# A two-layer encoder step on one core: GpSimd decodes the picks of the first two units, part of the projections is written beside the first dots, and the modulation weights are spread through the first attention

## The chip, the cores and the metric

The kernel runs on one core of a Trainium2 chip. The metric is the device time of one execution in microseconds. Five engines work side by side, each on its own list of instructions in order: TensorE (PE), VectorE (DVE), ScalarE (ACT), GpSimd (POOL) and SyncE (SP), which here does nothing but issue transfers. They wait for one another through semaphores.

## What is computed

Two encoder layers over 512 prompt rows and 64 sample rows, width 1024. The first layer has latent attention, the second band attention; each is followed by an expert layer in which every row picks 128 of 16384 experts (8 heads, 16 each). The parts that matter here:

```python
mod = silu(c) @ ada_w[layer] + ada_b[layer]          # shifts, scales, gates of every norm
q = rmsnorm(c_q @ w_uq);  k, v = from ckv_all @ w_ukv # 16 heads
x = x + g_m * (softmax(q k^T) v @ w_o)

def peer_ffn(h, w_q, subkeys, u, v):                  # once per 128 rows and layer
    q = (xb @ w_q).reshape(128, 8, 2, 64)
    s = einsum('nhpe,hpke->nhpk', q, subkeys)         # 128 scores per half
    top_s, top_i = lax.top_k(s, 16)                   # per head and half
    cand_s = top_s[:, :, 0, :, None] + top_s[:, :, 1, None, :]   # 16 x 16
    best_s, best_pos = lax.top_k(cand_s, 16)
    idx = take_along_axis(cand_i, best_pos)           # the expert's number
    g = softmax(best_s)
    a = gelu(einsum('nd,nhkd->nhk', xb, u[idx]))
    return einsum('nhk,nhkd->nd', g * a, v[idx])
```

## The kernel before

**Units.** The rows fall into five tiles (the sample's 64 rows first, then four prompt tiles of 128), and a tile in a layer is a unit: units 0 to 9. Each unit goes through attention (`attention`), the scores of the experts (`select`, `prepare`), the choice of the experts on DVE (`choose`), 64 (sample) or 128 gathered rows of `u` with one dot product each on DVE (`gather_u` on POOL into four slots of 0.5 MB, `dot` on DVE), and as many gathered rows of `v`, which PE adds up (`gather_v`, `add_values`). A gather may be issued when the dot that used its slot four rows earlier is done.

**Steady stages.** From the end of the ramp on, stage by stage, the dots of one unit stand beside the values of the unit before, the choice of the next and the attention of the one after.

**The ramp.** What comes before that is ordered by `RAMP` (line 54), a string that every engine walks through letter by letter. Each letter names a generator; an engine runs its next piece of that generator, if it has one. The letters are: l, one 2 MB piece of the modulation weights `ada_w` (PE multiplies it, line 626; DVE adds biases after each fourth, line 1481); Q, the queries of the sample; a, b and h, the attentions of units 0, 1 and 2 (some 17 pieces of one head, and the output product after each second head, line 847); s and r, the expert scores of units 0 and 1; p, the projections to queries, keys and values of the blocks n = 3 to 6 (blocks 0 to 2 come before the ramp), eight pieces each; c and k, the choice for units 0 and 1; e and f, the exponentials for it; d, the 64 dots of unit 0; t, the turning of its expert numbers. `RAMP` has five parts: modulations and first attention, its scores, choice beside projections, dots beside the second attention, dots beside the choice of unit 1.

**The choice.** `choose` does per head: the best 16 of two times 128 scores and of their 256 sums (`choose_head`, lines 1636 to 1648, three pieces of some 2 us). After two heads `decode` turns the 32 positions into expert numbers: it splits them (lines 1662 to 1665), then for each half compares them with `iota`, multiplies by the table of indices and sums (lines 1669, 1672, 1673: three instructions over 128 x 512). After four heads `name_experts` makes the list from which POOL gathers.

**The modulation weights.** `ada_w` comes in 28 pieces of 2 MB; 12 to 27 (the late ones) share two slots. SP issues piece p when piece p - 2 has been multiplied (`pieces`, a wait for `ada_used`). SP's list holds `pieces(12, 23)`, then the loads of the first attention. That attention's loads go by pairs of heads g: `keys(g+2)`, `values(g+1)`, `out_rows(g)` (0.5 MB of the output weights), and behind each of g = 0 to 4 one piece more, 23 to 27. The keys have two rings: `keys(g+2)` may be issued when the scores of pair g are done. All SP's transfers, these and the pieces, run in one queue (q1).

**Gathers.** POOL first stores the latents of the five tiles as they come (lines 1961, 1962), waits until all latents are multiplied (the gathered rows take the place of `w_in`), and then only gathers.

## Time and profile before

| | us |
|---|---|
| median of 3 runs | 4176.54 (4174.93 to 4184.52) |
| the profiled execution, its own time | 4168.8 |
| span of its trace | 4166.9 |

| engine | busy us | share of the span |
|---|---|---|
| PE | 2633.7 | 63% |
| DVE | 2452.3 | 59% |
| POOL | 2448.0 | 59% |
| ACT | 452.8 | 11% |

The transfers moved 1478 MB, 355 GB/s on average; the gathers' queue q0 alone had 75% of the sixteen DMA engines' time. How to read it: no engine is busy all the time, and the share of the transfers is an average over stages that differ much. So the stretches are looked at one by one.

### The profile page before, as it was taken

To read this page: it belongs to the slowest core of one execution; us is meant where nothing else is said; L and a number is where in the kernel's file an instruction comes from. 1 tells how busy PE (TensorE), PEld (TensorE's weight loads), DVE (VectorE), ACT (ScalarE), POOL (GpSimd) and SP (SyncE) were. 2 spreads that over 40 slices of the span, in tenths; PEclk is the share of its full clock that TensorE was granted. 3 is DMA by queue.
4 is the path that set the end of the run, shared out by engine and by line. 5 is a ranking of instruction groups with operands and counts; after the bars stand their busy time and mean duration, and the time that the engine had idled before them with its cause. 6 is when DMAs were issued, how large, how long until landed. Compare 5 with 4: busy or idle time off the path is not lost.

```text
span 4166.9 us, 31596 instructions
## 1 busy us (share of the span) xinstructions
PE 2633.7 (63%) x9649; PEld 958.8 (23%) x9649; DVE 2452.3 (59%) x5936; ACT 452.8 (11%) x1097; POOL 2448.0 (59%) x2323
## 2 busy tenths in 40 slices
PE   6587854664564455655465765656464677767789
PEld 2144532221222111211121222222121321111122
DVE  2119687786666556755773665677557667754410
ACT  2124411110010000110011011011001110000000
POOL 0000145777776757775676565556666677777776
PEclk8788866786787676767667877878686899999999
DMA  9761677999998999998998998899899999999999
GB/s 350 272 228 51 199 253 234 357 370 347 388 395 340 379 403 395 394 379 352 406 400 333 393 392 332 344 376 368 333 411 409 399 385 409 405 410 408 409 410 371
DMA packets 482966, 1478.16 MB, mean 355 GB/s; under 512 B 61568, under 2 KB 135248, under 8 KB 482128
## 3 DMA queue, kind: packets, MB, share of 16 engines
q0 software_dynamic: 332160, 1208.77, 75.0%
q1 hardware_dynamic: 125056, 255.33, 16.6%
q10 hardware_dynamic: 25584, 12.06, 1.0%
q8 instruction: 79, 1.29, 0.1%
q14 instruction: 87, 0.71, 0.0%
HBM read 1448.97 MB, written 28.57 MB: 355 GB/s over the span
## 4 chain that ended last, share of the span: by engine, by line
DMA 34%; POOL 23%; PE 18%; DVE 14%; issue 10%; ACT 1%; SPq 1%; ACTq 0%; DVEq 0%; POOLq 0%
DMA A<-in_uv,A 30%; POOL A L1930 12%; POOL A L1950 11%; PE P L939 8%; DVE A L1753 6%; DMA A<-in_ada_w 3%; PE P L847 2%; PE P L626 1%; PE P L881 1%; PE P L817 1%; PE P L687 1%; DVE A L1640 1%; DVE A L1637 1%; DVE A L1448 1%; PE P L804 1%
## 5 line engine op out<-in xcount | busy, mean ns | idle before, releaser
L939 PE MATMUL P<-A 128*32 128x512 f32 x4608 | 1314.2, 811 | 1185.5 <-DMA A<-in_uv,A 1117.5
L1930 POOL DMA_INDIRECT A<-in_uv,A x1152 | 1217.5, 1057 | 832.4 <-DVE A L1753 580.7
L1753 DVE CUSTOM_DVE_ANT_0 A<-A 128x1024 f32<-128x1024 f32 x900 | 1093.9, 1224 | 773.9 <-DMA A<-in_uv,A 766.4
L1950 POOL DMA_INDIRECT A<-in_uv,A x1152 | 1220.2, 1059 | 444.9 <-issue 320.2
L939 PEld LDWEIGHTS P<-A 128*32 128x32 f32 x4608 | 268.7, 132 | 2046.3 <-issue 1584.4
L1753 DVE CUSTOM_DVE_ANT_0 A<-P,A 128x1024 f32<-128x1024 f32 x252 | 307.8, 1224 | 263.0 <-DMA A<-in_uv,A 261.9
L956 PE MATMUL P<-A 128*128 128x512 f32 (+1 forms) x480 | 230.8, 627 | 18.5 <-DMA A<-in_w_kv 11.6
L817 PE MATMUL P<-A 128*128 128x128 f32 (+2 forms) x832 | 152.1, 317 | 87.1 <-DVE A L1603 82.6
L1961 POOL DMA_DIRECT2D out_ckv_p<-A x4 | 2.2, 548 | 333.9 <-DVE A L1528 333.9
L847 PE MATMUL P<-A 128*128 128x512 f32 (+1 forms) x320 | 190.9, 727 | 1.9 <-DMA A<-in_w_oA 1.3
L804 PE MATMUL P<-A 96*64 96x320 f32 (+9 forms) x320 | 148.5, 564 | 28.2 <-DMA A<-kBp_scratch 13.0
L831 PE MATMUL P<-A 128*64 128x128 f32 (+2 forms) x832 | 134.1, 295 | 38.2 <-ACT A L1263 38.1
L817 PEld LDWEIGHTS P<-A 128*128 128x128 f32 (+2 forms) x832 | 119.8, 210 | 154.9 <-DVE A L1603 98.6
L881 PE MATMUL P<-A 128*128 128x512 f32 x288 | 131.7, 612 | 0.0
L1271 ACT COPY A<-P 128x128 f32<-128x128 f32 (+3 forms) x160 | 62.7, 392 | 609.7 <-PE P L817 609.0
L956 PEld LDWEIGHTS P<-A 128*128 128x128 f32 (+1 forms) x480 | 85.9, 189 | 176.5 <-issue 127.8
L626 PE MATMUL P<-A,cs 128*32 128x512 f32 x448 | 76.9, 822 | 65.8 <-DMA A<-in_ada_w 65.8
L831 PEld LDWEIGHTS P<-A 128*64 128x64 f32 (+1 forms) x832 | 92.0, 150 | 69.3 <-issue 54.4
L1448 DVE TENSOR_SCALAR A<-P,gain,modT 128x128 f32<-128x128 f32 (+1 forms) x160 | 50.6, 389 | 79.8 <-PE P L606 79.8
L1636 DVE MAX8 A<-A 128x8 f32<-128x128 f32 (+1 forms) x240 | 80.5, 336 | 27.3 <-ACT A L1319 24.0
L804 PEld LDWEIGHTS P<-A 64*128 64x128 f32 (+3 forms) x320 | 55.5, 220 | 177.1 <-issue 169.0
L1753 DVE DVE_READ_ACCUMULATOR2_ANT A<- 128x1 f32 x1152 | 94.8, 82 | 0.0
(177 smaller groups left out, 2127.5 us busy)
## 6 DMA issues: line engine op xcount, KB each, us to landing
A<-in_ada_w SPq DMA_DIRECT2D x28, 2048.0 KB, 9.3
A<-in_w_kv SPq DMA_DIRECT2D x80, 512.0 KB, 8.6
A<-in_uv,A POOLq DMA_INDIRECT x2304, 7.8
A<-in_w_oA SPq DMA_DIRECT2D x40, 512.0 KB, 7.0
A<-in_w_q SPq DMA_DIRECT2D x40, 512.0 KB, 8.2
A<-in_w_oB SPq DMA_DIRECT2D x40, 512.0 KB, 7.9
A<-in_p_w_q SPq DMA_DIRECT2D x2, 4096.0 KB, 15.8
G<-mod_scratch SPq DMA_DIRECT2D x8, 512.0 KB, 7.6
```

The source lines that it names most:

```text
L626: ins = pe.matmul(P[32 * q:32 * q + 32, mods_bank(g), :], csT[:, c, :], slot[:, q, ADA_BLOCK * (c % 2):ADA_BLOCK * (c % 2 + 1)], start=(c ...
L804: ins = pe.matmul(P[0:r, n % 2, 0:nk], lhs, rhs, start=True, stop=not masked, skip_group_check=True)
L817: ins = pe.matmul(P[0:size, 2, b * 128:b * 128 + r], probs[m % 2][0:r, b * 128:b * 128 + size], turner[m % 2][0:r, 0:r], start=True, stop= ...
L831: ins = pe.matmul(P[p0:p0 + 64, 3, 0:r], V[0:size, b, p0:p0 + 64], probT[m % 2][0:size, b, 0:r], start=(b == 0), stop=(b == len(bl) - 1), ...
L847: ins = pe.matmul(P[0:r, 4 + b, :], oT[:, c, 0:r], w_o[pair % 2][:, 512 * b:512 * b + 512], start=(c == 0), stop=(c == C - 1), skip_group_ ...
L881: ins = pe.matmul(P[:, b, :], hT[:, c, :], w_pq[:, c, 512 * b:512 * b + 512], start=(c == 0), stop=(c == C - 1))
L939: ins = pe.matmul(Y[32 * j:32 * j + 32, b, :], spread[:, w:w + STRIDE], row[:, 512 * b:512 * b + 512], start=(m == 0), stop=(m == STRIDE - ...
L956: ins = pe.matmul(P[0:r, bank + b, :], h[:, c, 0:r], mid_ring[n % 4][:, 512 * b:512 * b + 512], start=(c == 0), stop=(c == C - 1), skip_gr ...
L1448: ins = dve.tensor_scalar(dst[:, c, 0:r], P[:, b0 + c // 4, (c % 4) * 128:(c % 4) * 128 + r], gainv[:, s, NORM[kind], c:c + 1], modTv[:, s ...
L1753: dve.tensor_tensor_reduce(u_slot[b], row, u_slot[b], 1.0, 0.0, ALU.mult, ALU.add, dots[u % 2][:, j:j + 1]).then_inc(sem("dots_done"), 1)
L1930: pool.indirect_dma_start(u_slot[at % U_SLOTS], None, table, bass.IndirectOffsetOnAxis(ap=expert[u % 2][:, j:j + 1], axis=0)).then_inc(sem ...
L1950: pool.indirect_dma_start(row, None, table, bass.IndirectOffsetOnAxis(ap=expertT[u % 3][:, n:n + 1], axis=0)).then_inc(sem(name), 16)
```

## The change

Three things change, all of them in the ramp.

1. **GpSimd decodes.** For units 0 and 1 the choice is `choose_first`: DVE splits the positions and copies the indices (`split_ranks`), and POOL does the rest of `decode` in 14 instructions per pair of heads: for each half a subtraction, a comparison with zero, a product (128 x 512 each) and four additions that halve the rows (256, 128, 64, 32 elements). Every one but the last waits for the one before. DVE waits for pairs 0 and 1 ahead of its first `name_experts`, which now comes after the sixth head, and for pairs 2 and 3 ahead of the second. POOL uses 1024 elements that the second layer's bias strips take later.
2. **The order of `RAMP`.** POOL walks through `RAMP` too: its stores of the latents, its decodes and its gathers stand between one another. Before the first gather there are 20 pieces of the projections as before (POOL waits for the same latents), but 16 of them, not 24, stand in the part with the choice, and all of the choice is ahead of the first gather; the other 17 pieces stand beside the second attention and, but for the first four, beside dots.
3. **Pieces in the first attention.** SP holds 5 instead of 11 late pieces ahead of the first attention's loads, then two behind the first loads, and the others one by one behind the pairs (three behind pair 5). PE multiplies 3 instead of 9 ahead of the attention.

```diff
-RAMP = ["llllllQlll" + "aal" * 7 + "a" * 7, "spsssss", "ccp" * 8 + "e" + "ccp" * 7 + "cp" * 5 + "e" + "cp" * 3,
-        "bdp" * 9 + "bbd" * 6 + "t" + "rdddrdddrdddrdddrdddr", "kkddh" * 8 + "f" + "kkddh" * 8 + "kkkfddhkkk" + "hhhh"]
+RAMP = ["lQll" + "aal" * 7 + "al" * 6 + "a", "spsssss", "ccp" * 6 + "cpe" + "ccp" * 6 + "cpepc",
+        "bp" * 4 + "gbp" + "bdp" * 12 + "bbdd" * 2 + "t" + "rddd" * 5 + "r",
+        "kddh" * 10 + "kdh" * 3 + "f" + "kdh" * 6 + "k" * 7 + "f" + "dhdhdd" + "k"]
...
-            pieces(4 * EARLY, 4 * EARLY + 11)
+            pieces(4 * EARLY, 4 * EARLY + 5)
...
                 keys(1)
                 values(0)
+                if u == 0:
+                    pieces(4 * EARLY + 5, 4 * EARLY + 7)
                 for g in range(C):
...
                     out_rows(g)
-                    if u == 0 and g == 0:
+                    if u == 0 and g < C - 1:
+                        n = 4 * EARLY + 7
+                        pieces(*((n, n + 1), (n + 1, n + 2), (n + 2, n + 3), (n + 3, n + 4), (n + 4, n + 5), (n + 5, n + 8), (n + 8, n + 9))[g])
+                    if u == 0 and g == 2:
                         pass_mods(EARLY, EARLY + 2, "mods2")
                         biases_of_mods(EARLY + 2, ADA_GROUPS, "biases_loaded")
-                    if u == 0 and g < 5:
-                        pieces(4 * EARLY + 11 + g, 4 * EARLY + 12 + g)
...
+            def choose_first(k):
+                dve.wait_ge(sem("scores_copied"), k + 1)
+                for h in range(PH):
+                    if h == 6:
+                        dve.wait_ge(sem("heads_decoded"), 4 * k + 2)
+                        name_experts(0, k, 0)
+                        yield
+                    if h == 4:
+                        shift_best(0)
+                    yield from choose_head(h)
+                    if h % 2 == 1:
+                        split_ranks(h // 2)
+                shift_best(1)
+                yield
+                dve.wait_ge(sem("heads_decoded"), 4 * k + 4)
+                name_experts(0, k, 1)
+                yield
...
+            def decode(u, pair):
+                lo, hi = 2 * pair, 2 * pair + 2
+                at = slice(lo * TOPK, hi * TOPK)
+                ch, ht = spare
+                pool.wait_ge(sem("pairs_ranked"), PH // 2 * u + pair + 1)
+                for x in range(2):
+                    tab = indf[:, 2 * lo + x:2 * hi:2, :].unsqueeze(2)
+                    step(pool.tensor_tensor(ch.rearrange("p g k j -> p (g k) j"),
+                                            bc(iota[:, :].unsqueeze(1), [128, 2 * TOPK, TOPK]),
+                                            bc(pick[:, x, at].unsqueeze(2), [128, 2 * TOPK, TOPK]), ALU.subtract))
+                    step(pool.tensor_scalar(ch, ch, 0.0, None, ALU.is_equal))
+                    step(pool.tensor_tensor(ht, ch, bc(tab, [128, 2, TOPK, TOPK]), ALU.mult))
+                    rows = ht.rearrange("p g k j -> p (g k) j")
+                    for n in (8, 4, 2):
+                        step(pool.tensor_tensor(rows[:, :, 0:n], rows[:, :, 0:n], rows[:, :, n:2 * n], ALU.add))
+                    ins = pool.tensor_tensor(hsum[:, x, at].unsqueeze(2), rows[:, :, 0:1], rows[:, :, 1:2], ALU.add)
+                    if x == 0:
+                        step(ins)
+                ins.then_inc(sem("heads_decoded"), 1)
```

**SP's list at the first attention, before**, from the last load of pair 0's values on. `in_ada_w` is a piece of the modulation weights, `kAs_scratch`, `qA_scratch` and `vAs_scratch` are the keys, queries and values of a pair of heads, `in_w_oA` is a block of the output weights; the waits stand in brackets.

```order
L350 DMA A<-vAs_scratch 64x128
L350 DMA A<-kAs_scratch 96x2x320 [waits scores_ready]
L350 DMA A<-qA_scratch 96x2x64
L350 DMA A<-vAs_scratch 128x256
L350 DMA A<-vAs_scratch 64x128
L350 DMA A<-in_w_oA 128x1024
L350 DMA mod_scratch<-A 2x2x512 [waits mods_summed]
L350 DMA mod_scratch<-A 2x2x512 x3
L350 DMA modT<-mod_scratch 128x4x8 [waits mods2_stored]
L350 DMA modT<-mod_scratch 128x4x8
L350 DMA A<-in_ada_b 2x2x512 x4
L350 DMA A<-in_ada_w 128x4x1024 [waits ada_used]
```

**The same place in SP's list after**, from the last load of pair 0's values on.

```order
L352 DMA A<-vAs_scratch 64x128
L352 DMA A<-in_ada_w 128x4x1024 [waits ada_used] x2
L352 DMA A<-kAs_scratch 96x2x320 [waits scores_ready]
L352 DMA A<-qA_scratch 96x2x64
L352 DMA A<-vAs_scratch 128x256
L352 DMA A<-vAs_scratch 64x128
L352 DMA A<-in_w_oA 128x1024
L352 DMA A<-in_ada_w 128x4x1024 [waits ada_used]
L352 DMA A<-kAs_scratch 96x2x320 [waits scores_ready]
```

What moved: eleven pieces stood ahead of the attention's first load, now five do; the other six went between its loads, and the loads of pairs 2 and up now stand behind pieces 17, 18, 19 and so on.

**PE's list at the start of the first attention, after** (line 631 is a piece of the modulation weights, 809, 822 and 836 are the scores, the turning and the values of a head, 852 is the output product of a pair).

```order
L717 MATMUL P<-ident,A 96x64 x16
L631 MATMUL P<-A,cs 32x512 x16
L809 MATMUL P<-A 64x320 x2
L631 MATMUL P<-A,cs 32x512 x8
L809 MATMUL P<-A 64x320
L822 MATMUL P<-A 128x64 x2
L822 MATMUL P<-A 64x64
L809 MATMUL P<-A 64x320
L822 MATMUL P<-A 128x64 x2
L822 MATMUL P<-A 64x64
L836 MATMUL P<-A 64x64 x3
L631 MATMUL P<-A,cs 32x512 x8
```

At the same place of PE's list before (626, 804 and 712 are what 631, 809 and 717 are after):

```order
L712 MATMUL P<-ident,A 96x64 x16
L626 MATMUL P<-A,cs 32x512 x24
L804 MATMUL P<-A 64x320 x2
L626 MATMUL P<-A,cs 32x512 x8
L804 MATMUL P<-A 64x320
```

So PE multiplies piece 15, not piece 21, after the first two heads, and one piece more after each two heads and, at the end, after each.

**POOL's list behind the last latents, after** (lines 2014 to 2022 are a decode, one half; 1965 is a gather of `u`).

```order
L2003 DMA out_ckv_p<-A 128x256
L2004 DMA out_kr_p<-A 128x32
L1965 DMA A<-in_uv,A 128x1024 x47
L2014 TENSOR_TENSOR A<-iota,A 128x512
L2017 TENSOR_SCALAR A<-A 128x512
L2018 TENSOR_TENSOR A<-A 128x512
L2021 TENSOR_TENSOR A<-A 128x32x8
L2021 TENSOR_TENSOR A<-A 128x32x4
L2021 TENSOR_TENSOR A<-A 128x32x2
L2022 TENSOR_TENSOR A<-A 128x32
```

**And before**, with nothing between the gathers of units 0 and 1:

```order
L1961 DMA out_ckv_p<-A 128x256
L1962 DMA out_kr_p<-A 128x32
L1930 DMA A<-in_uv,A 128x1024 x66
L1979 MEMSET A 128x2080
L1950 DMA A<-in_uv,A 128x1024
```

The decodes of unit 1 now stand between the gathers of unit 0: one behind 47 of them, one ten gathers later, two behind the sixty-fourth. The decodes of unit 0 stand ahead of the first gather, between the stores.

## Rows read from the trace of the kernel before

**Rows 1.** Stretches: length, busy PE, PEld, DVE, ACT, POOL; clock, DMA share, GB/s

```profile
202.00:281.00 79.00, 72.49 (x368) 31.74 (x368) 17.23 (x52) 15.78 (x73) 0.00 (x0) 0.86 0.71 244
...
314.00:431.00 117.00, 88.91 (x291) 52.13 (x292) 106.09 (x319) 48.02 (x106) 3.45 (x7) 0.87 0.17 49
431.00:522.00 91.00, 69.56 (x277) 43.38 (x275) 55.74 (x125) 39.93 (x98) 17.89 (x18) 0.85 0.70 224
522.00:559.00 37.00, 21.72 (x92) 12.49 (x92) 23.35 (x44) 8.75 (x14) 17.56 (x15) 0.77 0.89 309
559.00:688.00 129.00, 69.25 (x224) 45.18 (x224) 119.72 (x372) 19.32 (x62) 49.61 (x38) 0.68 0.67 216
688.00:3997.00 3309.00, 2001.41 (x7220) 672.49 (x7220) 2080.55 (x4934) 269.47 (x640) 2241.30 (x2114) 0.79 0.99 380
```

**Rows 2.** SP's issues in the first attention: start, us to issue, transfer

```profile
135.90 57.74 SPq L350 DMA_DIRECT2D A<-in_ada_w  x11
...
207.54 1.39 SPq L350 DMA_DIRECT2D mod_scratch<-A  x4
...
213.98 0.39 SPq L350 DMA_DIRECT2D A<-in_ada_w  x1
...
216.68 0.58 SPq L350 DMA_DIRECT2D A<-in_w_oA  x1
217.31 0.43 SPq L350 DMA_DIRECT2D A<-in_ada_w  x1
...
248.11 0.43 SPq L350 DMA_DIRECT2D A<-in_ada_w  x1
```

**Rows 3.** Chain of waits, the landing of piece 23: start, us, what

```profile
213.98 7.63 DMA A<-in_ada_w
```

**Rows 4.** The transfer of `w_oA` that was issued at 216.68: us from issue to landing

```profile
DMA to landing us min/median/max: 7.6/7.6/7.6
```

**Rows 5.** PE in the first attention: start, us, line, idle before and what ended it

```profile
202.27 2.37 PE L804 MATMUL P<-A 96*64 96x320 f32 x4 [9.04 <-DMA A<-qA_scratch]
...
211.63 1.92 PE L626 MATMUL P<-A,cs 128*32 128x512 f32 x16
213.48 0.75 PE L804 MATMUL P<-A 96*64 96x320 f32 x2
...
217.79 3.56 PE L847 MATMUL P<-A 128*64 128x512 f32 x4
...
242.79 1.33 PE L804 MATMUL P<-A 96*64 96x320 f32 x2
...
253.83 2.72 PE L626 MATMUL P<-A,cs 128*32 128x512 f32 x16
```

**Rows 6.** DVE's decode, 314 to 689: line, shape, count, busy us, mean ns, idle before

```profile
L1672 DVE TENSOR_TENSOR A<-A 128x512 f32<-128x512 f32 x16 | 11.1, 692 | 0.5
L1669 DVE TENSOR_TENSOR A<-iota,A 128x512 f32<-128x512 f32 x16 | 11.0, 689 | 0.4
```

**Rows 7.** POOL: a memset of 512 elements, the first gather, two gathers later

```profile
0.99 0.53 POOL L1954 MEMSET A<- 128x512 f32 x1
...
430.75 1.32 POOL L1930 DMA_INDIRECT A<-in_uv,A  x1 [0.30 <-issue]
...
564.25 1.68 POOL L1930 DMA_INDIRECT A<-in_uv,A  x1 [4.03 <-DVE A L1753]
566.23 0.94 POOL L1930 DMA_INDIRECT A<-in_uv,A  x1 [0.30 <-issue]
```

**Rows 8.** PE in block n = 5: its keys, and its latents

```profile
393.42 4.67 PE L659 MATMUL P<-A 128*128 128x512 f32 x8
...
416.50 9.28 PE L687 MATMUL P<-A 128*128 128x384 f32 x32 [0.47 <-ACT G L1195]
```

**Rows 9.** DVE: the residual after the first attention, and a dot

```profile
279.32 1.22 DVE L1629 TENSOR_TENSOR X<-X,A 64x1024 f32<-64x1024 f32 x1
...
563.89 1.22 DVE L1753 CUSTOM_DVE_ANT_0 A<-A 128x1024 f32<-128x1024 f32 x1
```

62 lines of the change are left out of this document (56 added, 6 removed).

## The prediction

> **What bounds the kernel now.** I read the stretches first [rows 1]. From 688 us to 3997 us the DMA engines are busy 0.99 of the time; the last 170 us are values still to be added. Nothing of that part is changed, so a microsecond won or lost ahead of 688 is one at the end. Ahead of it DVE is the fullest engine of 314 to 431 (106.1 of 117 us) and of 559 to 688 (119.7 of 129), and in 431 to 522 nothing is full (DVE 55.7, PE 69.6 of 91): there the chain PE, ACT, DVE of one projection block sets the pace. In 202 to 281, the first attention, PE is busy 72.5 of 79 us.
>
> The sum is made against the profiled execution, 4168.8 us (span 4166.9); the median of the runs shown is 4176.5, and I add the difference to that.
>
> **Pieces in the first attention.** Start with the queue. Eleven pieces were issued in 57.7 us [rows 2], 5.8 us each with the one ahead still in transfer; issued into an idle queue one lands after 7.6 us [rows 3]. The loads of a pair of heads follow it in the same queue: `w_oA` issued 2.7 us after piece 23 landed 7.6 us later [rows 2, 4], so 10.3 us after the piece was issued; the keys and queries, 0.3 of those 1 MB, by about 8.4.
>
> Before, the loads of pair g+2 stood ahead of the piece that follows, and PE needed them two groups of heads later. After, piece 19+g may be issued only when piece 17+g has been multiplied, which PE does after heads 2g+4 and 2g+5, and the keys of pair g+3 stand behind that wait; the very next heads, 2g+6 and 2g+7, need them. So transfers and PE take turns, five times (pairs 2 to 6):
>
> - SP issues the piece, and the keys land 8.4 us later; the piece itself is not what is waited for, its predecessor has long landed.
> - PE then does two heads, the output product and one piece: from 213.5 to 221.4 the two heads and the product [rows 5], and 1.9 the piece, 9.8 us. At the lower clock the same four take from 242.8 to 256.5, 13.7 us. I take 9.8.
> - 18.2 us a turn. If the product too takes the 1.9 us of the piece, 16.6; at the lower clock, 22.1.
>
> Before, a turn took (248.1 - 217.3)/3 = 10.3 us [rows 2].
>
> Timeline: the first keys land some 8.6 us after piece 16 is issued, as 202.3 is 8.6 after 193.6 [rows 2, 5]. Five pieces instead of eleven put that 6 x 5.8 = 35 us earlier, at 168. Pieces 15 and 16 are multiplied by 174 and by 168 + 11.3 = 179.5 (213.5 less 202.3, [rows 5]). Piece 18 is issued then, behind 17, and lands at 187.3, the keys of pair 2 at 188; PE is through with pair 2 at 198. Four more turns, 73 us, and 1 us for the storing of the modulations that now stands ahead of pair 5's keys (6.4 us, 207.5 to 214.0, mostly beside piece 21): 272. Pair 7's keys, head 14 and piece 22: 12.5 us, 284.5. Then pieces 24 to 27 with two slots: 24 at 284.5, 25 at 292 (head 15, a product and a piece), 26 at 296; the last values and `w_oA` block 6 land behind 26 at 307.5, piece 27 is issued at 313 and lands at 320.5, the last `w_oA` block at 322, its product and piece 27 take 4 us, DVE's two residual instructions 2.5 us: 329. Before it was 280.5 [rows 9]. **Term 1: +48 us**, from 317 (+36) to 353 (+73) with the turns at 16.6 and 22.1.
>
> **Scores of unit 0**, 281 to 314: same instructions, the first blocks of `p_w_q` still come before PE wants them. 0.
>
> **Choice and projections to the first gather.** Before 117 us (313.6 to 430.75, [rows 7]); both versions wait for the same latents. DVE's decode is three instructions of some 11 us per 16 halves, 33 us [rows 6], 4.1 us a pair, 4.3 with the gaps. Ahead of the first gather 3 of 4 pairs had been decoded: DVE loses 13 us of its 106, and gains 3 us for four heads of the second attention. 96 us are left. Three pairs' decodes on POOL stand beside heads; the fourth can't: between its positions and `name_experts` DVE has two projection pieces, some 5 us. How long does POOL take? The trace shows no such instruction. From below: six of 512 elements at the 0.53 us of the memset [rows 7], eight small ones at 0.3: 5.6 us. From above: a gather took 1.68 us when a dot was running and 0.94 when none was [rows 7, 9]; if each of the 14 waits for one 1.22 us instruction of DVE, 14 x 1.8 = 25 us. I take 13, about half of them held up. DVE waits 8 us there. After it, pieces 17 to 20 (block n = 5 from its keys to its latents) run as the bare chain of PE, ACT and DVE. It took from 393.4 to 425.8 before, with DVE's heads beside it [rows 8]; I take that 32 us for it again. The work of DVE in it is some 18 us of the 96, so 14 are idle. 96 + 8 + 14 + 2 for POOL's own order = 120. **Term 2: +3 us**, from -11 (the cover is full) to +15.
>
> The Trainium skill speaks against this move: GPSIMD Engine Reference, section 3.1, has a 2048-element fp32 tensor_tensor at 4497 ns against 2293 on VectorE. An estimate from it is about 12 us for a pair, and the sum would be the same within 1 us. SBUF - State Buffer, section "SBUF: two separate sides", calls the port pair of the two engines an exclusive lock against a VectorE instruction with two SBUF inputs; by that rule the trace agrees (1.68 against 0.94 us), and it would push the decode to its upper end.
>
> **Second attention and its scores.** 431 to 522 before, 91 us, and 37 us more to 559. Four heads of the attention have moved ahead of the first gather, and four projection pieces (21 to 24, the second half of block 5) have come in; the other nine pieces and nine of the heads stand as before. By the 8 us a piece of rows 8 the four pieces would cost 32 us, by what DVE does in them 4; the four heads that went, and the six that now stand between pieces instead of behind them, give that back in part. I take them as equal, the middle of what I can bound. **Term 3: 0**, from -15 to +15: nothing is full here, so a finer interleave can give something, and the load of `w_pq` (now issued some 22 us ahead of its use instead of 25) can cost something.
>
> **Dots beside the choice of unit 1**, 129 us, DVE 93% full. Four decodes go: -17 us. But POOL now decodes between gathers. While it does, DVE has four gathered rows; two thirds of a head, four dots and some heads of the attention cover 14 us, a decode and the 7 us to the next landing take 20. That is 6 us of waiting for the first decode, 3 for the second (fewer dots per piece there), none for the third (no dots stand there), and 6 for the fourth, which DVE waits for itself with four dots as its cover. **Term 4: -17 + 15 = -2 us**, from -15 to +35 with the decode at 6 and 25 us. Queued behind each decode on POOL are the gathers of rows 48, 58 and of unit 1; they start late but DVE's order asks for no more.
>
> Sum: +48 + 3 + 0 - 2 = **+49 us**: 4217.8 for the profiled execution, 4225.5 against the median.
>
> **Rivals.**
>
> A. *The first attention gains.* If the queue stays full: 16 pieces at 5.8 and eight pairs' loads at 2.7 us are 114 us from 136, and with 7 us for the end of the chain the residual is done at 257, 23 us earlier. With the rest at its middle: -22 us, 4154. For it: DMA was 0.71 busy in 202 to 281. Against: the order of SP's waits, which leaves nothing in the queue while PE is at work.
>
> B. *The turns cost half.* Turns at 12 to 13 us (say the loads overlap the piece better), +25 us, and terms 2 to 4 near their lower ends, -25: no change, 4176. It is the reading in which DVE's relief is worth its 30 us in full.
>
> C. *POOL is the bound.* The decodes take 25 us: term 2 +15, term 4 +35, with term 1 as above: +98, 4275. It decides from about 20 us a pair, where two heads and their projections (20 us) no longer cover one. The port speaks for it; that most of DVE's work in a head is on one input speaks against.
>
> D. *The change doesn't move what bounds*: if the gathers after 688 made up for a late start. They don't: 0.99 busy leaves 33 us in 3309.
>
> **The numbers.** Main forecast 0.62, A 0.13, B 0.15, C 0.09, D 0.01. Time 4225. The main forecast's own range is 4200 to 4255 (+25 to +80). Below it B and part of A: from 4162 to 4256 about 0.2 is left out, most of A and C. A measurement of this kernel tells a difference from about 0.3%, 12.5 us. Faster by more: A and a fifth of B, 0.16. Within: most of B, 0.13. Slower: 0.71.
>
> **What would show it.** SP's issues of pieces 19 to 23 some 18 us apart (10 would be A), each right behind a piece on PE; DMA share near 0.5 in 180 to 320 instead of 0.85; `mixed` of unit 0 at 329; the first gather at about 482; POOL's 14 instructions 13 us a pair; DVE idle some 8 us at the last `name_experts` of unit 0; the ramp's end near 737 instead of 688, and from there the same 3479 us. I am wrong if pieces and keys of one pair overlap PE's work on the pair before, or if the second attention's stretch shrinks by tens of microseconds.

## The result, and the profile of the changed kernel

The changed kernel takes 4274.18 us (median of 4 runs, 4263.5 to 4291.69) against 4175.74 us for the kernel before in the same session: a ratio of 1.0237, with a 95% interval of 1.0199 to 1.0276. Its profiled execution took 4263.5 us (span 4261.5) against 4168.8, so 94.7 us more. The forecast was 49 us more, with a range that ended at 4255. The direction was right, the size half of what came.

Six moments of the ramp, in us from the start of each trace, divide it. The "residual" is the end of DVE's last instruction of an attention (`mixed`), "first best-16" the first MAX8 of a unit's choice, "ramp's end" the 65th dot, the first one of unit 1.

| moment | before | after | later by | its stretch: before | after | forecast for the stretch |
|---|---|---|---|---|---|---|
| residual of unit 0 | 280.5 | 351.9 | 71.4 | | | +48 |
| first best-16 of unit 0 | 313.6 | 384.6 | 71.0 | 33.1 | 32.7 | 0 |
| first gather | 430.8 | 527.5 | 96.7 | 117.1 | 142.9 | +3 |
| residual of unit 1 | 522.0 | 609.4 | 87.4 | 91.2 | 81.9 | |
| first best-16 of unit 1 | 559.3 | 650.2 | 90.9 | 37.4 | 40.9 | 0 for this and the row above |
| ramp's end | 688.1 | 782.7 | 94.6 | 128.8 | 132.4 | -2 |

The spans differ by 94.6 us too. Behind the ramp nothing is lost and nothing comes back, as the stretches of after show: length, busy PE, PEld, DVE, ACT and POOL, then granted clock, DMA share, GB/s.

```profile
136.00:167.00 31.00, 10.26 (x65) 2.82 (x66) 5.68 (x9) 2.56 (x5) 0.00 (x0) 0.61 1.01 381
167.00:352.00 185.00, 109.72 (x464) 45.13 (x464) 18.73 (x54) 16.05 (x73) 0.00 (x0) 0.67 0.46 165
...
385.00:483.00 98.00, 68.20 (x218) 40.21 (x218) 83.11 (x271) 38.25 (x78) 51.61 (x60) 0.84 0.17 48
483.00:527.50 44.50, 29.96 (x104) 19.13 (x104) 20.07 (x51) 23.34 (x51) 1.14 (x3) 0.73 0.19 59
...
782.50:4091.50 3309.00, 1996.33 (x7219) 666.38 (x7219) 2079.84 (x4930) 266.58 (x636) 2260.95 (x2118) 0.79 0.99 381
```

The last row is as long as the last of [rows 1], 3309 us, at the same clock and DMA share. The attention that took 79 us at a DMA share of 0.71 and a clock of 0.86 now takes 185 us, at 0.46 and 0.67: neither the transfers nor TensorE is full. And ahead of the first gather a stretch of 44.5 us has come in where nothing is full: DVE 20 us, PE 30, the DMA engines 0.19.

**The turns.** SyncE's issues in the first attention (start, us to issue, transfer):

```profile
199.35 0.38 SPq L352 DMA_DIRECT2D A<-in_ada_w  x1
199.78 0.51 SPq L352 DMA_DIRECT2D A<-kAs_scratch  x1
...
222.82 0.38 SPq L352 DMA_DIRECT2D A<-in_ada_w  x1
...
244.23 0.38 SPq L352 DMA_DIRECT2D A<-in_ada_w  x1
254.41 0.32 SPq L352 DMA_DIRECT2D A<-kAs_scratch  x1
...
270.79 0.38 SPq L352 DMA_DIRECT2D A<-in_ada_w  x1
...
292.22 0.38 SPq L352 DMA_DIRECT2D A<-in_ada_w  x1
```

TensorE over one of these turns (start, us, line, shape; in brackets the idle time before and what ended it):

```profile
197.06 2.22 PE L631 MATMUL P<-A,cs 128*32 128x512 f32 x16
209.08 1.33 PE L809 MATMUL P<-A 96*64 96x320 f32 x2 [9.80 <-DMA A<-qA_scratch]
...
212.80 1.33 PE L809 MATMUL P<-A 96*64 96x320 f32 x2
...
216.52 3.67 PE L852 MATMUL P<-A 128*64 128x512 f32 x4
220.12 2.63 PE L631 MATMUL P<-A,cs 128*32 128x512 f32 x16
```

Read the two together. A piece is issued at 199.35, since TensorE has just finished the one two ahead; behind it come the keys, and TensorE stands still for 9.80 us until they are there. Then it does two heads, the product and a piece, to 222.75, and the next piece is issued at 222.82. So far this is the mechanism as forecast. But a turn is 23.5, 21.4, 26.6 and 21.4 us long, not 18.2. TensorE's part takes 13.7 us here and 12.7 to 13.6 in the others: the scores of a head take 1.33 us here and took 0.75 at 213.48 in the kernel before [rows 5]; the product takes 3.67, and 1.93 in r9, where TensorE has not rested (below). The granted clock from 222.8 to 244.2 is 0.60, so most of the time the lower of its two levels, 1.2 GHz. The third turn has 4 us more, because the modulations are stored between the piece at 244.23 and the keys at 254.41.

**The choice.** GpSimd's timeline in the choice of unit 0: the first half of the first decode, and three rows from the second half of the next:

```profile
407.60 1.07 POOL L2014 TENSOR_TENSOR A<-iota,A 128x512 f32<-128x512 f32 x1
408.76 1.50 POOL L2017 TENSOR_SCALAR A<-A 128x512 f32<-128x512 f32 x1
410.35 1.27 POOL L2018 TENSOR_TENSOR A<-A 128x512 f32<-128x512 f32 x1
411.70 1.63 POOL L2021 TENSOR_TENSOR A<-A 128x256 f32<-128x256 f32 x3
413.41 0.24 POOL L2022 TENSOR_TENSOR A<-A 128x32 f32<-128x32 f32 x1
...
428.65 1.81 POOL L2017 TENSOR_SCALAR A<-A 128x512 f32<-128x512 f32 x1
430.54 1.78 POOL L2018 TENSOR_TENSOR A<-A 128x512 f32<-128x512 f32 x1
432.39 3.14 POOL L2021 TENSOR_TENSOR A<-A 128x256 f32<-128x256 f32 x3
```

A pair takes 12.2 us undisturbed (407.60 to 419.8) and up to 14.8 in this choice (445.52 to 460.3); in that of unit 1, where dots run beside it, the last pair takes 16.5 (761.20 to 777.7). The forecast had 13. What DVE waited for between 385 and 785, us in total, times, longest:

```profile
DVE A L1788 <- DMA A<-in_uv,A: 30.3, 15, 6.1
...
DVE A L1698 <- POOL A L2022: 17.0, 2, 10.4
...
DVE stat L1531 <- ACT stat L1154: 10.0, 1, 10.0
```

The 10.0 us in the third row and 7.6 us before a head of the second attention fall into the bare stretch from 483 to 527: pieces 17 to 20 of the projections, with nothing of the choice beside them. ScalarE in that stretch, three rows of it, and behind them the row of the kernel before that does the same as the second:

```profile
495.44 0.37 ACT L1286 ACTIVATE A<-P,stat 128x128 f32<-128x128 f32 x1 [4.26 <-DVE stat L1617]
495.80 1.50 ACT L1109 ACTIVATE A<-P,modT,gain 128x128 f32<-128x128 f32 x4
...
506.16 1.28 ACT L1117 ACT_TABLE_LOAD   x1
```

```profile
404.71 1.50 ACT L1104 ACTIVATE A<-P,modT,gain 128x128 f32<-128x128 f32 x4 [4.56 <-PE P L676]
```

L1109 scales what TensorE has turned for the projections, and TensorE had turned it by 490.0 (its row is 488.87, 1.12 us). It began at 495.80, because the exponential of a head (L1286) stood ahead of it in ScalarE's list and waited for DVE. In the kernel before no head stands there, and the same instruction began as the turning ended (404.7), where in after 5.8 us went by. ScalarE also loads a table six times between 485 and 527, 1.28 us each, since exponentials and square roots take turns; before's same pieces, from 393 to 430, have none.

### The profile page after: what moved, and what is told of

It reads as the page before. It is cut to its first block, busy times and chain, and to the rows that moved or that the text cites. A ratio compares the mean times of both kernels' runs of the same rounds, so it can differ in the third digit from the quotient of the medians.

```text
span 4261.5 us, 31667 instructions
## 1 busy us (share of the span) xinstructions
PE 2646.6 (62%) x9649; PEld 960.8 (23%) x9649; DVE 2431.3 (57%) x5888; ACT 460.0 (11%) x1103; POOL 2561.0 (60%) x2435
## 4 chain that ended last, share of the span: by engine, by line
DMA 33%; POOL 25%; PE 18%; DVE 13%; issue 10%; ACT 1%; SPq 1%; ACTq 0%; DVEq 0%; POOLq 0%
DMA A<-in_uv,A 28%; POOL A L1965 12%; POOL A L1985 11%; PE P L944 8%; DVE A L1788 5%; PE P L852 2%; DMA A<-in_ada_w 1%; PE P L631 1%; DMA A<-qA_scratch 1%; PE P L822 1%; PE P L809 1%; PE P L886 1%; DVE A L1453 1%; PE P L836 1%; DVE A L1642 1%
## 5 line engine op out<-in xcount | busy, mean ns | idle before, releaser
L961 PE MATMUL P<-A 128*128 128x512 f32 (+1 forms) x480 | 233.8, 628 | 24.3 <-DMA A<-in_w_kv 15.9
L852 PE MATMUL P<-A 128*128 128x512 f32 (+1 forms) x320 | 204.9, 774 | 23.4 <-ACT A L1268 17.1
L1617 DVE TENSOR_REDUCE stat<-P 64x1 f32<-64x320 f32 (+4 forms) x80 | 38.7, 484 | 142.1 <-PE P L809 121.7
## 6 DMA issues: line engine op xcount, KB each, us to landing
A<-in_w_kv SPq DMA_DIRECT2D x80, 512.0 KB, 8.6
A<-in_w_oA SPq DMA_DIRECT2D x40, 512.0 KB, 7.5
A<-in_w_q SPq DMA_DIRECT2D x40, 512.0 KB, 8.0
A<-in_w_oB SPq DMA_DIRECT2D x40, 512.0 KB, 7.9
G<-mod_scratch SPq DMA_DIRECT2D x8, 512.0 KB, 7.7
```

Source lines behind the costliest of these rows:

```text
L852: ins = pe.matmul(P[0:r, 4 + b, :], oT[:, c, 0:r], w_o[pair % 2][:, 512 * b:512 * b + 512], start=(c == 0), stop=(c == C - 1), skip_group_ ...
L961: ins = pe.matmul(P[0:r, bank + b, :], h[:, c, 0:r], mid_ring[n % 4][:, 512 * b:512 * b + 512], start=(c == 0), stop=(c == C - 1), skip_gr ...
```

## The experiments

The stretch behind the ramp took 3478 to 3497 us in the traces of some sessions and 3600 to 3629 in those of others, and the medians of the kernel before differ likewise (4170 to 4176 and 4304 to 4310 us), so each ratio below is against the kernel before in the same session. The ramp doesn't show that difference (the residual of before is at 280.5 in one kind of session, that of r1, with the same first attention, at 281.1 in the other), so its moments are compared across all traces. There is one trace for each kernel; seven kernels that share the same new first attention (r3, r5, r6, r7, r10, r11, r14) have its residual between 265.3 and 279.4 us; the granted clock of its 98 to 108 us was 0.90 in r7, 0.81 in r6 and 0.82 in r3. So a difference of less than some 10 us at one moment says little, and the later stretches are taken from the residual on. There kernels of one order agree better: before, r4 and r7 lie within 0.6 us of one another at the ramp's end, the six in the changed order (after, r1, r3, r8, r9, r13) within 7.8.

| kernel | residual 0 | first gather | residual 1 | ramp's end | residual 0 to first gather | residual 0 to ramp's end | ratio to before (95%) |
|---|---|---|---|---|---|---|---|
| before | 280.5 | 430.8 | 522.0 | 688.1 | 150.2 | 407.6 | 1 |
| after | 351.9 | 527.5 | 609.4 | 782.7 | 175.6 | 430.8 | 1.0237 (1.0199 to 1.0276) |
| r1 | 281.1 | 457.7 | 540.0 | 715.5 | 176.7 | 434.4 | 1.0031 (1.0008 to 1.0055) |
| r2 | 353.7 | 534.6 | 616.6 | 783.9 | 180.9 | 430.2 | 1.0193 (1.0164 to 1.0222) |
| r3 | 273.4 | 448.6 | 527.1 | 700.0 | 175.2 | 426.6 | 1.0009 (0.9984 to 1.0034) |
| r4 | 351.5 | 503.3 | 593.2 | 758.5 | 151.8 | 407.0 | 1.0156 (1.0139 to 1.0173) |
| r5 | 279.4 | 431.9 | 522.1 | 694.5 | 152.4 | 415.0 | 1.0007 (0.9986 to 1.0027) |
| r6 | 274.7 | 428.9 | 516.1 | 689.1 | 154.2 | 414.4 | 1.0009 (0.9992 to 1.0026) |
| r7 | 265.3 | 415.5 | 507.1 | 672.7 | 150.2 | 407.4 | 0.9998 (0.9979 to 1.0016) |
| r8 | 557.4 | 734.5 | 814.7 | 986.8 | 177.1 | 429.4 | 1.0744 (1.0712 to 1.0775) |
| r9 | 352.2 | 528.0 | 606.5 | 779.6 | 175.8 | 427.4 | 1.0206 (1.0178 to 1.0234) |
| r10 | 269.5 | 428.9 | 515.2 | 685.4 | 159.4 | 415.9 | 1.0014 (0.9996 to 1.0031) |
| r11 | 278.4 | 428.7 | 522.3 | 687.6 | 150.3 | 409.2 | 0.9981 (0.9960 to 1.0003) |
| r12 | 353.3 | 557.1 | 635.4 | 856.5 | 203.8 | 503.2 | 1.0393 (1.0361 to 1.0425) |
| r13 | 343.1 | 518.4 | 599.0 | 773.0 | 175.3 | 429.9 | 1.0190 (1.0162 to 1.0218) |
| r14 | 269.1 | 412.9 | 512.0 | 674.7 | 143.8 | 405.6 | 0.9982 (0.9968 to 0.9997) |

### r1 and r4: the first attention undone, and the first attention alone

r1 is the changed kernel with `RAMP`'s first part and SyncE's list as before; r4 the kernel before with the changed ones.

```diff
-RAMP = ["lQll" + "aal" * 7 + "al" * 6 + "a", ...
+RAMP = ["llllllQlll" + "aal" * 7 + "a" * 7, ...
...
-            pieces(4 * EARLY, 4 * EARLY + 5)
+            pieces(4 * EARLY, 4 * EARLY + 11)
...
```

> The changed kernel with the old first attention put back: eleven pieces ahead of its loads, the other five behind the pairs. In the trace of after the residual of unit 0 was done 71.3 us later than in before. Theory 1 (the turns in the first attention cost 71 us, and nothing behind them makes up for it): 4274 - 71 = 4203 us, with `mixed` of unit 0 back at about 281 us, the first gather at 281 + 33 + 143 = 457 us, and about 27 us above before. Theory 2 (the later start is partly covered by what stands behind, so that putting it back gives back only part): between 4220 and 4274 us.

> The kernel before with the new first attention alone (five pieces ahead, the others one by one). Theory 1 (the cost of the turns is the same whatever stands behind): 4176 + 71 = 4247 us, `mixed` of unit 0 at 352 us. Theory 2 (what stands behind it in before's order, with more of DVE's work in it, hides a part, or is held up further): more than 10 us off that.

Measured: the residual of unit 0 falls to 281.1 in r1 and rises to 351.5 in r4. The ramp's end moves by 67.2 and 70.4 us, the time of r4 by 1.56%, some 67 us. Both as theory 1 has it: 71 us, whatever stands behind. r1's first gather, at 457.7, and its ramp's end, 27.4 us behind before's, are as expected too; its ratio, 3 to 24 us above before, is a little under the 27.

### r3: the same transfers, one pair of heads ahead

```diff
-                if u == 0:
-                    pieces(4 * EARLY + 5, 4 * EARLY + 7)
...
-                    if u == 0 and g < C - 1:
-                        n = 4 * EARLY + 7
-                        pieces(*((n, n + 1), (n + 1, n + 2), ...)[g])
-                    if u == 0 and g == 2:
+                    if u == 0:
+                        pieces(4 * EARLY + 5 + g, 4 * EARLY + (6 + g if g < C - 1 else 16))
+                    if u == 0 and g == 4:
```

> The changed kernel with one thing different: in SyncE's list each single piece of ada_w stands one pair of heads later, so that the keys of pair g + 2 are issued ahead of the piece that waits for pair g (piece 17 + g behind the loads of g, the last four behind pair 7, the modulations stored behind g = 4). The same transfers, the same list on TensorE. Theory 1 (the 22 us turns come from the order of the waits: nothing is in the queue while TensorE works): the turns shrink to 10 to 12 us, `mixed` of unit 0 falls from 352 to between 257 and 275 us, and the time to 4274 - 77 to 4274 - 95 = 4179 to 4197 us. Theory 2 (transfers of 2 MB and the pairs' loads get in each other's way, or TensorE's lower clock is what stretches the turns): turns of 17 us or more, `mixed` later than 310 us, the time above 4230 us.

Measured: residual at 273.4, 78.5 us earlier than after, with the same list on TensorE and the same bytes. SyncE in r3:

```profile
192.06 0.43 SPq L352 DMA_DIRECT2D A<-in_ada_w  x1
192.54 0.50 SPq L352 DMA_DIRECT2D A<-kAs_scratch  x1
...
199.99 0.43 SPq L352 DMA_DIRECT2D A<-in_ada_w  x1
200.47 0.51 SPq L352 DMA_DIRECT2D A<-kAs_scratch  x1
...
209.70 0.43 SPq L352 DMA_DIRECT2D A<-in_ada_w  x1
```

Pieces come 8 to 10 us apart, and from 167 to 273 the DMA engines are busy 0.78 of the time instead of 0.46. So neither the size of the pieces nor their number is what cost 71 us; it is that the keys stood behind a wait for work that TensorE finishes just before it needs those keys. (The storing of the modulations moved back with the pieces, from g = 2 to g = 4; in after it makes one turn some 4 us longer.) Even so the fine interleave is worth little over before's eleven in one go: 273.4 against 280.5, and 272.8 on average over the seven kernels that have it.

### r8, r9 and r13: TensorE kept busy in the turns

```diff
                     ins.then_inc(sem("ada_used"), 1)
+                    if 4 * EARLY + 5 <= p < 4 * EARLY + 9:
+                        pe.wait_ge(sem("mods_summed"), g)
+                        for i in range(10):
+                            pe.matmul(P[:, 13 - mods_bank(g), :], ident[:, :], w_in[:, i % 8, 0:512], start=True, stop=True, skip_group_check=True)
                     yield
```

This is r13. r9 has 13 of them behind each of the pieces 15 to 20, r8 there 52 of `P[0:32, ...]` with 32 columns of `csT`.

> The changed kernel, with 52 more matmuls of 32 x 512 behind each of the pieces 15 to 20 on TensorE, into an unused bank and behind the signal that the piece is used; their results go nowhere. They fill the wait for the keys. At 2 us for 16 they take 6.5 us at full clock and up to 9.5 at the lower one, so they fit into the idle 8.7 us or stand over by 1. Theory 1 (TensorE, idle for 9 us a turn, comes back at the lower granted clock, and two heads, product and piece take 13.7 us instead of 9.8): the turns fall from 22.5 to about 19 us, `mixed` of unit 0 from 352 to about 335, the ramp's end from 783 to about 766. Theory 2 (the clock there has another cause): turns of 22 us or more, `mixed` at 352 or later.

> As r8_te_kept_busy, with a price from the right row: a 128 x 512 product of one output block takes 0.48 us at full clock and 0.91 at the lower one (x4 in 1.93 and 3.67), and 13 of them stand behind each of the pieces 15 to 20, 6.3 us at full clock, inside the 8.7 us of idle. Their results go nowhere. Theory 1 (TensorE comes out of 9 us of idleness at the lower granted clock, and that is 3.9 us of each turn): the turns fall from 22.5 to 18.5 to 19.5 us, `mixed` of unit 0 from 352 to 332 to 338, the ramp's end from 783 to 763 to 769. Theory 2 (the lower clock there has another cause): turns of 22 us or more.

> The changed kernel with ten additional 128 x 512 products on TensorE behind each of the pieces 17 to 20, 8.8 us at full clock by r9 (26 passes in 11.43 us), so no longer than the idle time they fill; their results go nowhere. Theory 1 (the turn is 8.5 us for the keys and TensorE's part, which takes 13.7 us because of the lower clock alone, 7.9 at full clock): turns of 16.5 to 17.5 us, `mixed` of unit 0 at 328 to 333 us instead of 352, everything behind it earlier by as much, ramp's end 759 to 764. Theory 2 (something else stretches the turns, and the 19.4 us of r9 had another reason): turns above 20 us, `mixed` later than 342.

r8 shows no shorter turn: its additional matmuls took 44.8 us behind each piece, and the turns became 53 us. I had priced them by the row of a piece. It does tell of the clock: with TensorE never idle, two heads, product and piece took 7.9 us in three of its turns (326.38 to 334.29, and the same from 379.01 and 431.65), and 9.6 and 9.7 in the other two, at whose product the lower clock came for some 4 us. r9's took 11.43 us, twice what I had expected, since a row of the trace counts two passes for each such product; they were some 2 us longer than the gap, and the first of them (behind piece 15) stood where there was no gap. Its residual stayed at 352.2 instead of 332 to 338. But its turns say what the clock is worth. TensorE in r9:

```profile
200.39 0.75 PE L815 MATMUL P<-A 96*64 96x320 f32 x2
...
204.69 1.93 PE L858 MATMUL P<-A 128*64 128x512 f32 x4
206.55 1.92 PE L631 MATMUL P<-A,cs 128*32 128x512 f32 x16
208.41 11.43 PE L639 MATMUL P<-A,ident 128*128 128x512 f32 x26
219.76 0.75 PE L815 MATMUL P<-A 96*64 96x320 f32 x2
```

Two heads, product and piece take 8.0 us here (200.39 to 208.41) and 13.7 in after; the turn is 19.4 us, though the filling is longer than the wait it fills. The same 44 us of both kernels, r9 first (columns as in the first fence):

```profile
203.00:247.00 44.00, 44.00 (x182) 19.13 (x180) 4.24 (x15) 4.60 (x22) 0.00 (x0) 1.00 0.40 141
```

```profile
203.00:247.00 44.00, 26.54 (x96) 11.55 (x96) 4.14 (x13) 3.96 (x18) 0.00 (x0) 0.61 0.38 133
```

In r13 the pieces 19 to 23 are issued at 202.6, 224.0, 240.8, 267.5 and 284.4: two turns take 16.8 and 16.9 us, as theory 1 says, and two 21.4 and 26.7. In the first of the latter TensorE was 1.55 us without work before its keys came, ran the scores and the turning of a head at full clock and then fell to the lower one (1.33 us for the scores of the next at 215.18); in the second it had been idle for 4.57 us behind the stored modulations. The residual is at 343.1, 8.8 us earlier than after, not the 20 expected. So the lower clock accounts for some 5 us of each turn. Where the filling left a gap behind it, be it 1.55 us, the lower clock came back; so it did in r9 behind the one gap of its turns, 1.92 us ahead of 260.50. A gap is not the only occasion, though: in r8 TensorE had no idle time from 171.2 on, and yet from 276.4 to 280.0 the granted clock was 0.53 and the product took 3.58 us. Such a fall without a gap lasted some 4 us where it was seen (also in r9 at 287.4 and in before at 217.8); what brings it on is open.

### r5 and r6: four projection pieces back beside the choice

```diff
-"ccp" * 6 + "cpe" + "ccp" * 6 + "cpepc", "bp" * 4 + "gbp" + "bdp" * 12 + ...
+"cpccp" * 4 + "cpe" + "cpccp" * 4 + "cpepc", "b" * 4 + "gbp" + "bdp" * 12 + ...
```

r6 has `"gbbp" + "bbdp" * 3 + "bdp" * 9` in place of `"b" * 4 + "gbp" + "bdp" * 12`. Both have r3's first attention.

> The changed kernel with the pieces ahead (as r3_pieces_ahead), and the first four projection pieces of block n = 5 (17 to 20) put back beside the choice of unit 0 instead of behind it: 19 of them there, not 15, and bare heads of the second attention in front of the first gather. GpSimd still decodes. Theory 1 (the 25 us that stand between the residual of unit 0 and the first gather too much come from that bare chain): 175 us becomes 148 to 155, so the ramp ends at 700 - 20 to 700 - 27 = 673 to 680 us, ahead of before's 688. Theory 2 (DVE is slowed by GpSimd's decodes, and the order has little to do with it): the stretch stays above 168 us and the ramp ends at 693 or later.

> As r5_twenty_pieces, and the first gathers and DVE's steps of the second attention change places: no head of it ahead of the first gather. Theory 1 (DVE and TensorE spend some 8 us on four heads there that would fit beside dots): first gather 5 to 10 us earlier than in r5, the ramp's end 0 to 8 us earlier. Theory 2 (the projections and not the gathers set the end of that part, since block 5 and 6 must be through before the choice of unit 1): the first gather earlier, but the ramp's end within 3 us of r5.

Measured from the residual to the first gather: 152.4 us in r5 where r3 has 175.2, 2 us from before's 150.2. That is theory 1: the 25 us come and go with where the four pieces stand. With them beside the choice DVE waits for no decode of unit 0 either, though the decodes are the same, so the 10.4 us of waiting belong to the placement too. Of the 22.8 us r5 gives 11 back later: residual to ramp's end is 415.0 against 426.6, and the end is at 694.5, not 673 to 680. Half of what the four pieces cost ahead of the gather they save behind it. The times, 1.0007 and 1.0009 of before's, don't show the rest. r6 is within 1 us of r5 from the residual to the ramp's end, its theory 2, and its first gather came no earlier.

### r2, r10 and r11: who decodes

r2 is the changed kernel, r11 is r10, each with DVE doing the decode in `split_ranks` and GpSimd none. r10 is r3 with the projections and dots where before has them:

```diff
-"ccp" * 6 + "cpe" + "ccp" * 6 + "cpepc", "bp" * 4 + "gbp" + "bdp" * 12 + "bbdd" * 2 + "t" + ...
+("cpcpcpccp" * 2 + "cpcp") + "cpe" + ("cpcpcpccp" * 2 + "cpcp") + "cpecp", "g" + "bdp" * 9 + "bbd" * 6 + "t" + ...
```

> The changed kernel in all its order, but DVE decodes the picks of units 0 and 1 itself, at the place where it would have handed them to GpSimd. Theory 1 (GpSimd's decodes are worth next to nothing here: they take 4.1 us a pair off DVE, 33 us in all, and give back 17 us of waits and some 10 to 15 us by which DVE's own instructions are stretched while GpSimd works): within 10 us of 4274, so 4264 to 4284. Theory 2 (the relief of DVE counts in full): 4274 + 33 = 4307 us. Theory 3 (GpSimd is what is waited for, decodes and held-up instructions): clearly faster than 4264.

> Pieces ahead (as r3_pieces_ahead), GpSimd decodes, and the projections where before had them: 24 of 33 pieces by the end of the choice of unit 0, and before's order of the dots beside the second attention. Theory 1 (only the placement of the projections cost time, and with before's placement GpSimd's decodes take their share off a full DVE): from the residual of unit 0 to the first gather 140 to 148 us instead of before's 150, and from the residual to the ramp's end 395 to 405 instead of 407.6. Theory 2 (the waits for GpSimd and the stretching of DVE's instructions eat the relief): 407 to 420 us.

> As r10_tight_gpsimd, with the decode on DVE at the place of the handing over. With r10 it gives the price of GpSimd's decodes where DVE is full. Theory 1 (relief counts where DVE is full): 10 to 20 us longer than r10 from the residual of unit 0 to the ramp's end. Theory 2 (as in the changed kernel, where both came out alike): within 5 us of r10.

r2: from the residual to the ramp's end 430.2 us where the changed kernel has 430.8. Eight decodes on another engine and nothing gained at that moment; the ratios, from two sessions, are 1.0193 for r2 and 1.0237, with intervals that overlap. Where they went can be read off. DVE's groups in r2 between 387 and 786, the dots, the three instructions of the decode and the turner of a head (line, shape, count, busy us, mean ns, idle before):

```profile
L1795 DVE CUSTOM_DVE_ANT_0 A<-A 128x1024 f32<-128x1024 f32 x66 | 79.5, 1222 | 18.0 <-DMA A<-in_uv,A 17.2
L1759 DVE TENSOR_TENSOR A<-iota,A 128x512 f32<-128x512 f32 x16 | 11.1, 692 | 0.6
L1762 DVE TENSOR_TENSOR A<-A 128x512 f32<-128x512 f32 x16 | 11.1, 692 | 0.5
L1763 DVE TENSOR_REDUCE A<-A 128x32 f32<-128x512 f32 x16 | 11.0, 686 | 0.5
...
L1608 DVE TENSOR_SCALAR A<-ident,stat 128x128 f32<-128x128 f32 x32 | 9.2, 286 | 1.1
```

And in the changed kernel, between 385 and 785, the dots and the turner:

```profile
L1788 DVE CUSTOM_DVE_ANT_0 A<-A 128x1024 f32<-128x1024 f32 x66 | 82.8, 1270 | 31.1 <-DMA A<-in_uv,A 30.3
L1608 DVE TENSOR_SCALAR A<-ident,stat 128x128 f32<-128x128 f32 x32 | 11.6, 361 | 1.1
```

DVE is relieved of 33.2 us. Against it stand some 12 us by which its other instructions of the same forms got longer (3.2 of them in the dots, 2.4 in the turners), 17.0 us of waits for GpSimd, and 13.1 us more of waits for gathered rows (30.3 less 17.2), since GpSimd can't issue gathers while it decodes.

r10 against r11, where DVE is as full as it was before: 415.9 and 409.2 us. So GpSimd's decodes cost some 7 us there, theory 2 of r10. The times of the two, ten runs each in one session, agree: medians of 4308.86 and 4299.23 us. In r10 DVE waits 9.0 us for the last decode and 32.2 us for gathered rows; in r11 none and 9.6.

### r12: each decode twice

```diff
-                for x in range(2):
+                for i in range(4):
+                    x = i % 2
```

> The changed kernel with each of GpSimd's decodes done twice, the second time over the first. One takes 12.1 us alone and up to 14.8 beside DVE. Theory 1 (the last decode of each choice is already what is waited for, by 10.4 and 6.6 us, and two decodes follow each other without a gap at the end of unit 1's choice): +12 to +26 us at the first gather, +12 to +28 more in the choice of unit 1, so the ramp ends at 783 + 24 to 783 + 54 = 807 to 837 us. Theory 2 (the waits seen are slack that another resource would fill anyway): less than +15 us in all.

Measured: 28 us more at the first gather (203.8 against 175.6), 44 more from there to the ramp's end, at 856.5. That is beyond theory 1's upper end of 837. Not the last decode alone is waited for: ahead of the first gather DVE waits twice, 36.5 us in all, and in unit 1 the gathers stand behind the earlier decodes as well. DVE's waits for GpSimd are 67.2 us instead of 17.0, those for gathered rows 54.4 instead of 30.3.

### r14 and r7: only the three decodes that nothing waits for, and none

r10 with GpSimd decoding pairs 0 to 2 of unit 0, and DVE the other five.

> As r10_tight_gpsimd, but GpSimd decodes only the first three pairs of unit 0; DVE decodes the last pair of unit 0 and all of unit 1. Theory 1 (GpSimd's decodes cost where something waits for them: the last pair, by 9 us, and the gathers of unit 0 behind unit 1's decodes, by 23 us; the other three are free relief): residual of unit 0 to the first gather 144 to 150 us, to the ramp's end 398 to 406 instead of r11's 409. Theory 2 (the first three cost DVE as much, in stretched instructions, as they take off it, or the projections' chain sets that part): 406 to 413 us.

Measured: 143.8 us from the residual to the first gather, 6.4 less than before and 6.5 less than r11, and 405.6 to the ramp's end, 2.0 and 3.6 less. DVE doesn't wait for GpSimd at all, and 9.9 us for rows. Behind the first gather it loses most of it again: the second attention takes 99.0 us instead of 91.2, and 93.5 in r11. The time is 0.9982 of before's, with an interval that just leaves one out (0.9968 to 0.9997), 7.5 us less: the fastest of these kernels by its ratio together with r11, and the only one whose whole interval lies below before. Not all of it is the decodes': r14 has the new first attention too, and of the 13.4 us by which its ramp ends before that of before 11.4 are the residual's. What the three decodes give by themselves at the ramp's end is within the spread of the traces. r7 is the kernel before with r3's first attention alone.

> The kernel before with the first attention of r3_pieces_ahead alone: five pieces of ada_w ahead of its loads, the others one pair later than in the changed kernel; the rest as before, DVE decodes. Theory 1 (additive): `mixed` of unit 0 at 273 us instead of 280.5, the ramp's end at 688 - 7 = 681 us, the time 7 us (0.17%) below before. Theory 2 (the 11 pieces in one go were as good): ramp's end 688 us or later.

Its ramp ends 15.5 us earlier in its trace, of which 15.3 are the residual; the ratio of 0.9998 (from 9 us below before to 7 above) doesn't show that much. The 7 us expected can't be told from nothing.

## Why the prediction was wrong, by its own steps

**What bounds the kernel: right.** No microsecond of the ramp's 94.6 comes back or is added behind it. Rival D is out.

Two steps failed, one in term 1 and one in term 2, by 23 us each. Either alone would have left the forecast within its range.

**Term 1, +48 expected, 71 found: the mechanism right, one size off.** The failed step is "9.8 us" for TensorE's part of a turn. I read it from [rows 5], from a stretch of before in which TensorE had worked without a break since 202.27, and moved it into one in which it rests 9 us in every turn. The row for the other case stood beside it, 242.8 to 256.5, 13.7 us, and I named it and took the faster one. With it a turn is 22.1 us and the residual comes at 353; it came at 351.9, in turns of 21.4 to 23.5 and one of 26.6. Over the five turns from 177.3 to 292.2 TensorE's part took 66 us instead of 49, which is 17 of the 23 us. Another 3 are the storing of the modulations, which I had at 1 us and which made its turn some 4 us longer. The rest lies in the half pair behind the turns (15.5 us instead of 12.5) and in the wait, 8.5 to 9.7 us from issue to keys instead of 8.4. r8, r9 and r13 show that the lower clock makes the part as long as it is: with the gap filled the same part takes 7.9 to 8.0 us, and turns of 16.8 us appear. A chain that waits pays twice, once for the wait and once for the slower clock behind it.

**Scores of unit 0, 0: right** (32.7 against 33.1).

**Term 2, +3 expected, 25.7 found: wrong, outside its own bounds.** The failed step is the chain of pieces 17 to 20, "I take that 32 us for it again", with a smaller one in DVE's work ahead of it. I summed DVE's work as if it filled everything up to the bare chain, and added the chain. To the end of the last decode it took 98.3 us, where the sum had 96 - 18 + 8 + 2 = 88; DVE was busy 83 of them and waited 10.4 for GpSimd (8 expected). 6 us, by the same forms in r2, are instructions that got longer beside GpSimd, which I had costed at nothing for DVE though I had given GpSimd the delay of the shared port. The larger half is the chain: 44.5 us instead of 32. I took its 32 us from before, from 393.4 to 425.8, but that is where the matmuls of the latents end; the first gather came at 430.75 [rows 7], so before's chain is 37 us long, and some 5 of the 12.5 are this reading. And in before nothing of the second attention stood in it. Now four of its heads do, and TensorE, ScalarE and DVE reach them in order. I costed them by DVE's time alone, 3 us, and not as links of the chain; the rows of ScalarE above show one such link, 5.8 us, and the table loads. No run has the chain without the heads, so how the rest divides is read from the trace alone. r5 gives 22.8 of the 25 us back with the four pieces moved (and the bare heads left in front of the first gather), so the place of the pieces is shown to be the cause.

**Term 3, 0 expected, -5.8 found** (122.7 against 128.5 us), inside its bounds. The second attention gave 9.3 us, its scores took 3.5.

**Term 4, -2 expected, +3.7 found**, inside its bounds. DVE's busy time falls by 11.7 us (119.8 to 108.1), not by the 17 of the decodes, and there are 6.6 us of waiting for the last decode and the waits for rows.

**The price of a decode: the number right, by luck** (13 expected, 12.2 to 16.5 found). It was the middle of 5.6 and 25 us, "about half of them held up". But 12.2 us is the time with no instruction held up: one over 512 elements takes 1.05 to 1.5 us, not the 0.53 of the memset, and being held up adds 0 to 4 us a pair. r2 and r10 show the whole move to be worth from 0 to a loss of 7 us. By the Trainium skill's GPSIMD Engine Reference, section 3.1, the estimate for a pair was 12 us, and the trace agrees. Beside GpSimd's decodes DVE's dots take 1.27 us on average instead of 1.22 and 2.06 at the most, and GpSimd's own halving takes up to 4.20 us instead of 1.62: 12 us of DVE in 400. Where dots and a decode of unit 1 meet, the rows of the two engines, GpSimd's first, have to be read as one list:

```profile
688.81 2.06 POOL L2014 TENSOR_TENSOR A<-iota,A 128x512 f32<-128x512 f32 x1
...
690.96 2.35 POOL L2017 TENSOR_SCALAR A<-A 128x512 f32<-128x512 f32 x1
```

```profile
688.74 1.22 DVE L1788 CUSTOM_DVE_ANT_0 A<-A 128x1024 f32<-128x1024 f32 x1
...
689.89 2.06 DVE L1788 CUSTOM_DVE_ANT_0 A<-A 128x1024 f32<-128x1024 f32 x1
```

The first dot ends at 689.96. GpSimd's subtraction, 1.05 us long alone, ends 0.91 us later, at 690.87; the second dot, 1.22 us long alone, ends at 691.95, 1.08 us behind the subtraction; and GpSimd's comparison, 1.49 us long alone, ends at 693.31, 1.36 behind the dot. So the work of the two went one after another there, but for some 0.15 us. The Trainium skill's SBUF - State Buffer, section "SBUF: two separate sides", speaks of an exclusive lock; the trace agrees at these instructions. It cost only 12 us in all, since most of DVE's instructions in a choice kept their length: a best-16 over 128 scores (MAX8) took 0.29 us beside the decode as without it.

**Rival C** had 4275, and 4274 came, by another way: the decodes took 12 to 15 us, not 25. The near hit says nothing for it; r2 tells that taking all of them from GpSimd changes the ramp's end by 1 us.

## What to carry to other kernels

When a transfer waits for work that the engine finishes just before it needs the next load of the same queue, transfers and engine take turns; put the loads ahead of the wait, and the same bytes cost nothing (r3). When you price an engine's part in a chain with gaps, take the rows behind an idle time, not those of a full stretch, and count every instruction that stands in the chain's order as a link, also one that is cheap on the engine you look at. Hand work to GpSimd only where nothing waits for its end and it has no gathers to issue meanwhile: three decodes of eight were worth 6.5 us in their stretch (r14 against r11), of which 3.6 were left at the ramp's end, and the other five cost more than they gave (r10 against r14, 10.3 us).

## What the runs showed of the hardware

- In r8 104 matmul passes (52 products) of 32 columns by 512, all into the same 32 output partitions, took 44.8 us, 0.43 each; the 16 of a piece, which go to four groups of 32 partitions in turn, take 1.92 us, 0.12 each. So the row of a piece gave no price for one of its matmuls alone; that the four groups run side by side is my reading of it, and nothing but r8 bears on it.

```profile
225.63 1.92 PE L631 MATMUL P<-A,cs 128*32 128x512 f32 x16
227.37 44.80 PE L639 MATMUL P<-A,cs 128*32 128x512 f32 x104
```

- TensorE's clock: in r13 it had been idle for 9.8 us until 189.2, worked until 211.3, was idle for 1.55 us, ran from 212.87 to some 215 at full clock and then at the lower. In r9, with no idle time from 203 to 247, the granted clock was 1.00 throughout. In r8, with no idle time from 171.2 to 280.0, it was 0.97 up to 276.4 and 0.53 in the 3.6 us behind.
- On GpSimd the comparison of 512 elements with a constant takes 1.49 us, a subtraction of two inputs 1.05 and a product 1.26, where DVE does not hold them up. The form with one input is the slowest of the three.
